# Sums of squares of a second norm on four column quarters of the matrix array

## What is computed

```python
def rmsnorm(x, g):
    xf = x.astype(jnp.float32)
    y = xf * lax.rsqrt(jnp.mean(xf * xf, axis=-1, keepdims=True) + EPS)
    return (y * g.astype(jnp.float32)).astype(x.dtype)

h = h + rmsnorm(mix, g[1])
ff = conv_ffn(rmsnorm(h, g[2]), ffn_w_up[l], ffn_conv[l], ffn_w_down[l])
h = h + rmsnorm(ff, g[3])
```

## Time and profile before

| | us |
|---|---|
| median of 3 runs | 3407.08 |
| lowest and highest run | 3406.38, 3408.67 |
| span of the profiled execution, first to last instruction | 3404.4 |
| PE busy in that span | 3369.6 |
| DVE busy | 2516.7 |
| ACT busy | 1725.8 |
| mean granted PE clock, share of full speed | 0.998 |

### The profile page before, as it was taken

The page is one execution under the profiler, slowest core; times in us unless marked ns, Lnnn a source line. Parts: engine busy times, 40 slices in busy tenths (PEclk is TensorE's granted clock), DMA queues, the critical chain, the costliest instruction groups (busy, mean ns, idle before and its releaser), DMA issues. The chain is left out here.

```text
span 3404.4 us, 65711 instructions
## 1 busy us (share of the span) xinstructions
PE 3369.6 (99%) x25119; PEld 3147.0 (92%) x25119; DVE 2516.7 (74%) x3690; ACT 1725.8 (51%) x2638; POOL 124.3 (4%) x116
## 2 busy tenths in 40 slices
PE   9999999999999999999999999999999999999998
PEld 8998899989998989898899889999999998799987
DVE  6886888887887778787788865557786367777863
ACT  4563655545554545455545545446555344555552
POOL 0100202000200100000001000000000000000000
PEclk9999999999999999999999999999999999999999
DMA  4333223332233322222233321212223221123232
GB/s 142 111 105 112 88 88 104 111 111 94 99 105 111 105 79 84 78 83 92 69 104 105 113 99 63 72 59 69 100 92 106 93 77 39 43 75 100 94 104 81
DMA packets 89676, 311.33 MB, mean 91 GB/s; under 512 B 10816, under 2 KB 15296, under 8 KB 89472
## 3 DMA queue, kind: packets, MB, share of 16 engines
q1 hardware_dynamic: 89056, 307.19, 27.0%
q0 software_dynamic: 416, 1.29, 0.1%
HBM read 306.34 MB, written 2.10 MB: 91 GB/s over the span
## 5 line engine op out<-in xcount | busy, mean ns | idle before, releaser
L896 PE MATMUL ps<-x_hi,w_hi 128*128 128x264 f32 (+2 forms) x1840 | 571.9, 311 | 2.6 <-ACT pair L2884 0.9
L896 PE MATMUL ps<-x_hi,w_lo 128*128 128x264 f32 (+2 forms) x1840 | 562.1, 306 | 0.0
L896 PE MATMUL ps<-x_lo,w_hi 128*128 128x264 f32 (+2 forms) x1840 | 561.2, 305 | 0.0
L896 PE MATMUL ps<-h_hi,w_hi 128*128 128x264 f32 (+3 forms) x1282 | 406.8, 317 | 4.3 <-DVE h_lo L3209 1.9
L896 PE MATMUL ps<-h_hi,w_lo 128*128 128x264 f32 (+3 forms) x1282 | 395.8, 309 | 0.0
L896 PE MATMUL ps<-h_lo,w_hi 128*128 128x264 f32 (+3 forms) x1282 | 395.0, 308 | 0.0
L896 PEld LDWEIGHTS ps<-x_hi,w_hi 128*128 128x128 f32 x1840 | 346.4, 188 | 32.0 <-issue 10.2
L896 PEld LDWEIGHTS ps<-x_hi,w_lo 128*128 128x128 f32 x1840 | 347.0, 189 | 14.7
L896 PEld LDWEIGHTS ps<-x_lo,w_hi 128*128 128x128 f32 x1840 | 345.6, 188 | 15.8
L2993 DVE TENSOR_TENSOR w_lo<-raw,w_hi 128x1024 fp32r<-128x1024 f32 x214 | 260.8, 1230 | 107.4 <-ACT w_hi L1843 103.3
L997 PE MATMUL ps<-t_hi,w_hi 128*128 128x256 f32 x1152 | 322.7, 280 | 0.0
(11 more groups left out here) (425 smaller groups left out, 8817.2 us busy)
## 6 DMA issues: line engine op xcount, KB each, us to landing
raw<-wstream SPq DMA_DIRECT2D x577, 512.0 KB, 3.3
res<-xT SPq DMA_DIRECT2D x8, 256.0 KB, 6.7
out<-res SPq DMA_DIRECT2D x8, 256.0 KB, 2.4
near_bias<-consts POOLq DMA_DIRECT2D x1, 512.0 KB, 4.0
g_chunk<-consts POOLq DMA_DIRECT2D x1, 264.0 KB, 3.4
g_keep<-consts POOLq DMA_DIRECT2D x1, 256.0 KB, 3.2
par<-params SPq DMA_DIRECT2D x1, 232.5 KB, 7.5
far_bias<-consts POOLq DMA_DIRECT2D x1, 128.0 KB, 3.5
```

What stands on the lines that cost most here:

```text
L896: m = pe.matmul(ps[:, bank, 0:n], w[:, slot, wt, :], x[:, k, c0:c0 + n], start=first and q == 0, stop=last and q == 2)
```

## The change

For h = 1 at all sites and for h = 0 at sites 2 and 4, the eight products on the whole array become two blocks of four products. In a block, product j uses only 32 of `mean_w`'s columns and writes PSUM partitions 32j to 32j + 31, so that the four lie on four column quarters of the array; a block waits for its four squares at once and releases their buffers at once. After the second block ACT copies the bank into a square buffer, scaled by 32, and one product of the whole `mean_w` with that copy adds the four quarters and spreads the sum; `roots` waits for that product.

The places on PE change too. At h = 0 of sites 2 and 4 the blocks follow steps 21 and 27, and the adding product step 30. At h = 1, `between` becomes a table by k: at sites 1 and 3 the blocks and the adding product stand ahead of the x_lo products of k = 0, 2 and 4; at sites 2 and 4 the first block stands ahead of k = 6, the second block and the adding product behind k = 7. At h = 0 of sites 1 and 3 the products stay whole, and at site 3 four of them follow step 19 and four the last step (before: one each after 17, 19 and 21, five behind). Two semaphores that count set-up memsets become one. DVE's and POOL's orders stay.

```diff
     def inputs(*outs):
-        return dict(i=1, s=2 * KD, y=2 * KD, x=2 * KD) if outs else {}
+        return dict(i=1, o=2, s=2 * KD, y=2 * KD, x=2 * KD) if outs else {}
...
+        def in_quarters(st, h):
+            return h == 1 or st["halved"] > 1
+        def means_of(st, h):
+            return st["o0"] + (2 if h and st["halved"] > 1 else 0)
+        def part_buffer(st, h):
+            return square_buffer(st, h, SQUARES - 1)
...
-                ahead = (KD // 2 if st["kind"] == "glu2" else 0) if between else KD
...
                 for k in range(KD):
-                    if k == ahead:
-                        for f in between:
-                            f()
-                        between.clear()
+                    if k in between:
+                        between.pop(k)()
                     pe.wait_ge(s_xlo, x0 + k + 1)
                     for j in range(count):
                         product(0, j, k, w_hi, lo, False, k == KD - 1)
+                for k in sorted(between):
+                    between.pop(k)()
...
-                square_steps = (17, 19, 21) if halved == 1 else range(18, 18 + KD)
+                square_steps = {19: 0} if halved == 1 else {21: 0, 27: 1}
...
                                 if h and st.get("outs") and steps in square_steps:
-                                    squares_of(st, 0, [squared])
-                                    squared += 1
+                                    squares_of(st, 0, square_steps[steps])
+                                if h and st.get("outs") and halved > 1 and steps == 30:
+                                    mean_of(st, 0)
...
                 if st.get("outs"):
-                    between.append(lambda: squares_of(st, 1, range(KD)))
+                    first = 0 if halved == 1 else KD - 2
+                    between[first] = lambda: squares_of(st, 1, 0)
+                    between[min(first + 2, KD)] = lambda: squares_of(st, 1, 1)
+                    between[min(first + 4, KD + 1)] = lambda: mean_of(st, 1)
...
+            def squares_of(st, h, block):
+                if not in_quarters(st, h):
+                    for k in range(SQUARES * block, SQUARES * (block + 1)):
+                        pe.wait_ge(s_sqr, st["s0"] + KD * h + k + 1)
+                        pe.matmul(ps[:, 2 + h, 0:st["tok"] // 2], mean_w[:, :], square_buffer(st, h, k),
+                                  start=k == 0, stop=k == KD - 1).then_inc(s_sqp, 1)
+                    return
+                pe.wait_ge(s_sqr, st["s0"] + KD * h + SQUARES * (block + 1))
+                for j in range(SQUARES):
+                    rows = slice(FG * j, FG * j + FG)
+                    m = pe.matmul(ps[rows, 2 + h, 0:st["tok"] // 2], mean_w[:, rows],
+                                  square_buffer(st, h, SQUARES * block + j), start=block == 0,
+                                  stop=block == KD // SQUARES - 1, skip_group_check=True)
+                m.then_inc(s_sqp, SQUARES)
+            def mean_of(st, h):
+                pe.wait_ge(s_ms, means_of(st, h) + 1)
+                pe.matmul(ps[:, 2 + h, 0:st["tok"] // 2], mean_w[:, :], part_buffer(st, h), start=True, stop=True)\
+                    .then_inc(s_ms, 1)
             def renorm(st):
-                squares_of(st, 0, range(SQUARES, KD))
-                between.append(lambda: squares_of(st, 1, range(KD)))
+                squares_of(st, 0, 1)
+                between[0] = lambda: squares_of(st, 1, 0)
+                between[2] = lambda: squares_of(st, 1, 1)
+                between[4] = lambda: mean_of(st, 1)
...
-                roots(tok, (1, s_sqp, st["s0"] + 2 * KD, 3, s_root2, 4 * st["i0"] + 2))
+                roots(tok, (1, *mean_square(st, 1), 3, s_root2, 4 * st["i0"] + 2))
+            def mean_square(st, h):
+                if not in_quarters(st, h):
+                    return s_sqp, st["s0"] + KD * (h + 1)
+                act.wait_ge(s_sqp, st["s0"] + KD * (h + 1))
+                act.activation(part_buffer(st, h), ps[:, 2 + h, 0:st["tok"] // 2], ACT.Copy, scale=float(FG))\
+                    .then_inc(s_ms, 1)
+                return s_ms, means_of(st, h) + 2
...
-                past(act, s_sqp, st["s0"] + KD * h + (k + 1 - SQUARES if k >= SQUARES else 0))
+                past(act, s_sqp, st["s0"] + KD * h + (0 if k < SQUARES else SQUARES if in_quarters(st, h) else k + 1 - SQUARES))
```

More of the change, by code:

```diff
@@ L168, in plan @@
         f0=0,
+        o0=0,
     )
@@ L195, in inputs @@
     def inputs(*outs):
-        return dict(i=1, s=2 * KD, y=2 * KD, x=2 * KD) if outs else {}
+        return dict(i=1, o=2, s=2 * KD, y=2 * KD, x=2 * KD) if outs else {}
     def project2(units, chunks, lead, tok, after, *outs, early=0):
-        down("project2", units, chunks, lead, counts=dict(v=1, a=2 * KD, **inputs(*outs)), after=after, outs=outs,
+        counts = dict(v=1, a=2 * KD, **inputs(*outs))
+        if outs and LATE[len(chunks)] > 1:
+            counts["o"] = 4
+        down("project2", units, chunks, lead, counts=counts, after=after, outs=outs,
              tok=tok, early=early)
@@ L222, in plan @@
     outs = ("norm00",)
-    add("renorm", inputs(*outs), outs=outs, tok=T, lead=4)
+    add("renorm", inputs(*outs), halved=1, outs=outs, tok=T, lead=4)
     add("hgrn", dict(u=4 * KD, t=4 * KD, h=KD))
@@ L508, in build @@
         s_res = sem("s_res")
-        s_eps = sem("s_eps")
+        s_set = sem("s_set")
         s_win = sem("s_win")
@@ L529, in build @@
         s_mx = sem("s_mx")
-        s_idle = sem("s_idle")
         s_add = sem("s_add")
@@ L533, in build @@
         s_sqp = sem("s_sqp")
+        s_ms = sem("s_ms")
         s_y = sem("s_y")
@@ L914, in run_idle @@
             def run_idle(n):
-                pe.wait_ge(s_idle, 1)
+                pe.wait_ge(s_set, 1)
                 for _ in range(n):
                     pe.matmul(ps[:, 7, 0:2 * P], idle[:, 0:P], idle[:, :], start=True, stop=True)
-            late, between = [], []
+            late, between = [], {}
             def first_units(st, count, tok):
@@ L1246, in project @@
                 full = KD - halved
-                steps = squared = 0
-                square_steps = (17, 19, 21) if halved == 1 else range(18, 18 + KD)
+                steps = 0
+                square_steps = {19: 0} if halved == 1 else {21: 0, 27: 1}
                 for n in range(st["early"] if src != (att_hi, att_lo) else 0):
@@ L1285, in project @@
                                 if h and st.get("outs") and steps in square_steps:
-                                    squares_of(st, 0, [squared])
-                                    squared += 1
+                                    squares_of(st, 0, square_steps[steps])
+                                if h and st.get("outs") and halved > 1 and steps == 30:
+                                    mean_of(st, 0)
                             k0 += kn
-                if st.get("outs"):
-                    squares_of(st, 0, range(squared, KD))
+                if st.get("outs") and halved == 1:
+                    squares_of(st, 0, 1)
                 if st.get("scaled") or st.get("outs") and halved > 1:
@@ L1295, in project @@
                     if follower(st)["kind"] == "renorm":
-                        squares_of(follower(st), 0, range(SQUARES))
+                        squares_of(follower(st), 0, 0)
                     sums_of(st, parts(st) - 1)
                 if st.get("outs"):
-                    between.append(lambda: squares_of(st, 1, range(KD)))
+                    first = 0 if halved == 1 else KD - 2
+                    between[first] = lambda: squares_of(st, 1, 0)
+                    between[min(first + 2, KD)] = lambda: squares_of(st, 1, 1)
+                    between[min(first + 4, KD + 1)] = lambda: mean_of(st, 1)
             def sums_of(st, h):
@@ L2123, in project @@
                     act.wait_ge(s_res, KD)
-                    act.wait_ge(s_eps, 1)
+                    act.wait_ge(s_set, 2)
                 load_log_exp()
@@ L2702, in project2 @@
                     lead(2)
-                roots(tok, (0, s_sqp, st["s0"] + KD, 2, s_root2, 4 * st["i0"]))
+                roots(tok, (0, *mean_square(st, 0), 2, s_root2, 4 * st["i0"]))
                 for k in range(4):
@@ L2755, in renorm @@
                 root_of_layer, second_half = open_half
-                roots(st["tok"], (0, s_sqp, st["s0"] + KD, 2, s_root2, 4 * st["i0"]))
+                roots(st["tok"], (0, *mean_square(st, 0), 2, s_root2, 4 * st["i0"]))
                 root_of_layer()
@@ L2768, in renorm @@
                     second_half(k)
-                roots(st["tok"], (1, s_sqp, st["s0"] + 2 * KD, 3, s_root2, 4 * st["i0"] + 2))
+                roots(st["tok"], (1, *mean_square(st, 1), 3, s_root2, 4 * st["i0"] + 2))
                 for k in range(KD):
@@ L3011, in load @@
             def load(st):
-                dve.memset(idle[:, :], 0.0).then_inc(s_idle, 1)
```

(7 more changed lines are left out.)

## The result

The changed kernel takes 3422.8 us (median of 5 runs, 3421.4 to 3424.3) against 3407.1 (5 runs, 3406.4 to 3408.7): a ratio of 1.0045 with a 95% interval of 1.0035 to 1.0056, slower by 15.7 us. 3421.0 was forecast. The profiled execution of the changed kernel took 3421.4 us, 1.9 us above its own span of 3419.5.

The account below looks back on a forecast made before the run. PE is busy 3369.6 of 3404.4 us, but the order of waits at the four sites decides. Chain 8.2, half 0 0.7, sites 1 and 3 0.4 and clock 4.4 give 13.7 us on 3407.1: 3421, range 3412 to 3429.

Parts of the forecast that it names:

- The wait for x_lo: Half 1 of sites 2 and 4: PE waits 4.0 us ahead of k = 4 for DVE's late lows.
- The chain behind it: Half 1 of sites 2 and 4: blocks, squares, copy and adding product put logarithm and x_hi 4.09 us later a site.
- Half 0 of sites 2 and 4: Logarithm 1.08 us later, of which 0.36 comes through to PE at each site because DVE is late itself; twice, 0.7.
- Half 1 of sites 1 and 3: 0.2 us lost at each site, between 0 and 0.4, PE's saving going into waits for squares and x_lo.
- The clock: Sites 2 and 4: waits make the granted clock fall to half in part, costing 2.2 us a site, 4.4 together.
- Rival 3: The wait for x_lo is there but the clock holds at 1.00: 9.3 us slower, 3416.4; chance 0.20.
- price for the fall at site 1: Site 1 in the earlier trace: 3 us at half clock behind an idle wait of 2.19 us cost 1.5 us.
- Rival 1: PE's work decides, so its saving of 9.3 us makes the kernel faster, 3397.8 us; chance 0.03.
- Rival 2: Quarters run one after another, a block taking 1.80 us: 11.5 us more, 3432.3; chance 0.07.
- Rival 4: Stall real but partly made up where PE waits behind the sites: total under 0.2%, 6.8 us; chance 0.05.
- eight issues at an even pace: A block of quarters on PE: eight instructions issued each 0.055 us, 0.44 in all, taken as 0.48 us.

Follow-up runs that it names:

- place_alone: The kernel before with its whole products at half 1 of sites 2 and 4 moved behind x_lo of k = 5, no quarters; 3419.3 us, ratio 1.0035.
- lows_early: The changed kernel with DVE's lows of k = 4 to 7 moved ahead of its second half at sites 2 and 4; 3415.6 us, ratio 1.0027.
- fillers: The changed kernel with products nobody reads put into PE's two waits at half 1 of sites 2 and 4; 3418.8 us, ratio 1.0033.
- h0_whole: As lows_early, with half 0 of sites 2 and 4 back to eight whole products; 3414.1 us, ratio 1.0021.
- split1: The kernel before with half 1's whole products at site 1 in two groups of four, ahead of k = 0 and k = 2; 3406.7 us, ratio 0.9999.
- whole_lows_early: The kernel before, without quarters, with the edits of place_alone and lows_early together; 3406.9 us, ratio 0.9999.
- blocks_back: The changed kernel with both blocks of half 1 at sites 2 and 4 ahead of k = 4, adding product ahead of k = 5; 3413.5 us, ratio 1.0019.

## Why the prediction was right

**The wait for x_lo.** Forecast 4.0 us from the point where a next product would have started, and 4.01 by that count at site 2 (sixteen products of 0.121 behind 2353.91 end at 2355.85, and k = 4 starts at 2359.86); the idle time of the rows, 3.84 and 3.81, counts from the end of the last row. It is released by DVE's lows. place_alone brings it back without quarters and lows_early takes it away with them, so its cause is shown, not only read from rows.

**The chain behind it.** Forecast 4.09 a site at full clock; with the clock held up by fillers 4.31 and 4.27: 8.6 for 8.2. Squares 5 to 8 stood behind the block, the copy took 0.39 and the rest followed as written, and the 2.07 from logarithm to x_hi came back as 2.06 (2366.42 to 2368.48).

**Half 0 of sites 2 and 4.** Forecast 0.36, measured 0.4 each, and gone in h0_whole. PE stood there for the eighth square, 0.98 us at site 2, the logarithm came 1.16 later (forecast 1.08; 12.91 behind the last sum of the norm before it, against 11.75), and the rest of that lay under DVE's own delay as forecast. The rows of PE and ACT:

```profile
2341.02 0.42 PE L1354 MATMUL ps<-pair,mean_w 128*32 128x264 f32 x2 [0.98 <-ACT sums L2791]
...
2343.56 0.48 ACT L2771 ACTIVATE rstd<-ps,eps 128x264 f32<-128x264 f32 x1 [0.81 <-PE ps L1362]
```

**Half 1 of sites 1 and 3.** Forecast 0.2 each, at most 0.4; site 3 took 0.29. Site 1 took 0.83, outside the bound: there the clock fell inside the chain. In lows_early, where it fell near 2031, about as in the kernel before, the site took 18.61, 0.32 more than before. That is inside the bound: what the bound had left out is the clock. The 0.32 is itself a difference, 0.9 that the quarters cost and 0.5 that the placement brings (split1), which the forecast didn't part.

**The clock.** Forecast 4.4 at sites 2 and 4, measured 1.27 + 0.99 + 1.3 = 3.6; the runs of fillers are 4.0 us below the changed kernel's. The size was a guess near the middle of a wide range, so that it came this near is luck; that the clock falls in part was right. Rival 3, a clock that holds, is what fillers had to make by force. Its 1.3 behind site 4 have no counterpart behind site 2, where the stretch behind the logarithm's wait stayed at full speed. The prediction's price for the fall at site 1, 1.5 us for 3 us at half speed, doesn't show in that site's own interval: in place_alone's execution the clock stood at 1.00 there from 2030 to 2036, and the interval was 18.26, against 18.29 before with the fall.

**Sum.** 8.6 + 0.8 + 1.1 + 3.6 = 14.1, and 0.9 that the profiled execution of before had ahead of site 1: 15.0 of the span's 15.1. The forecast was 13.7. The clock's term was 0.8 too high, that of sites 1 and 3 was 0.7 too low and the chain's 0.4 too low; that these nearly cancel is luck. Against the medians 15.7 are measured; the 2 us between the forecast and these are within what either kernel's runs differ among themselves.

**The rivals.** Rival 1, PE's saving of 9.3 us, would have needed the lows to be there. lows_early put them there, and still nothing was gained, for the reason that whole_lows_early shows: at these sites PE has a microsecond to spare and the chain of squares and logarithm decides. Rival 2 falls with the rows of a block: 0.79 us, forecast 0.8. All four quarters use all rows of the array and start within 0.02 us of each other, and PEld's rows of the same block put the weight loads of the other four instructions at 2337.04 and 2337.05, while the first four run. The rule of the Trainium skill ("TensorE: Matmul & The Clock Gate", Part 3) that weight loads overlap running products only where the row group differs does not hold for these column groups. Rival 4, a total under 6.8 us, falls with the 15.7 measured.

## What to carry to other kernels

Cheaper products on the busiest engine are worth nothing at a spot where the next thing it needs comes from elsewhere; before moving work behind other work, read off when the inputs of that other work are written (here DVE's order, which is not in the diff at all, was worth 7 us with the quarters and 12 without). Batching four tiles into one instruction group makes the group wait for the last of the four and frees the buffers only together, which put a block, a copy and an addition into a chain that was the critical one. Where PE's clock falls behind a wait, the wait costs a second time (3.6 us here): count it, and where it matters try work that nobody reads.

## What was not expected of the hardware

The prediction took eight issues at an even pace for a block. The rows show two lots: four quarters start together, and the other four 0.25 us behind them at full clock (2337.01 and 2337.26), 0.45 at half clock (2361.85 and 2362.30). The sum hardly differs, 0.79 for 0.8, but a block's length goes with its columns, not with its eight issues. So it was in the earlier trace rows already: four instructions of 128 columns take 0.22 us and four of 272 take 0.46, in the ratio of the columns, so the 0.055 that the prediction took for the pace of issue was not one.

The clock's falls are less regular than the prediction's reading of the earlier trace rows. The same idle 2.1 us ahead of x_hi was followed by 0.50 at both sites in lows_early and at site 4 of the changed kernel, and by full speed at site 2 of the changed kernel, where the clock had already been at 0.50 until 2363 and was back. An idle 1.13 in whole_lows_early was followed by full speed. At site 1, the same code, with 2.18 to 2.19 idle ahead of half 0, was followed by a fall near 2030 in some executions, by one near 2042, behind waits of 1.07 and 0.89, in others, and by none in place_alone's; in blocks_back, which leaves site 1 as the change has it, that later fall lasted longer and the interval was 20.70 instead of 19.12. What decides between them stays open. Between the sites it is the same: somewhere from 2292 to 2299 the clock was at 0.50 in six of the nine profiled executions and at 1.00 in those of lows_early, fillers and split1, on code that is the same in all. From half 1 of site 1 to half 0 of site 2 split1 took 293.88 us, and the four other executions with whole products in that half 0, all with the fall, 295.37 to 295.50; with quarters there it is 294.43 and 294.45 without the fall (lows_early, fillers) and 295.84 and 295.94 with it (blocks_back, the changed kernel). So a fall goes with about 1.5 us there. Single executions of one kernel can thus differ by one or two microseconds, and that bounds what a profile of one execution can say.
